# Weight projections with the token columns read and written from last to first

## The reference

```
z   = h @ w_in                                   # 2048 x 11272
y_r = retention_out @ w_ret_proj                 # 1024 x 2048
y_f = attention_out @ w_fox_proj                 # 1024 x 2048
mix = (sigmoid(gr) * y_r + sigmoid(gf) * y_f) @ w_out
x1  = layer_norm(ALPHA * h + mix)
ffn = (silu(x1 @ w1) * (x1 @ w3)) @ w2           # inner width 5632
ple = sigmoid(x1 @ w_pg) * (p @ w_pe)
y   = layer_norm(ALPHA * x1 + ffn + ple)
```

## Time and profile before

| | |
|---|---|
| median of three runs | 1943.95 us (1942.95 to 1946.54) |
| span of the profiled execution, first to last instruction | 1944.3 us |
| TensorE matmul busy | 1859.9 us, 96% |
| VectorE busy | 1050.1 us, 54% |
| ScalarE busy | 793.6 us, 41% |
| GpSimd busy | 148.5 us, 8% |
| mean granted TensorE clock | 0.981 of full speed |

### The profile page before, as it was taken

The page is one execution under the profiler, slowest core; times in us unless marked ns, Lnnn a source line. Parts: engine busy times, 40 slices in busy tenths (PEclk is TensorE's granted clock), DMA queues, the critical chain, the costliest instruction groups (busy, mean ns, idle before and its releaser), DMA issues.

```text
span 1944.3 us, 39410 instructions
## 1 busy us (share of the span) xinstructions
PE 1859.9 (96%) x14346; PEld 1754.6 (90%) x14346; DVE 1050.1 (54%) x2097; ACT 793.6 (41%) x930; POOL 148.5 (8%) x262
## 2 busy tenths in 40 slices
PE   5999999999899999999978999999999999999996
PEld 4999998888777877889978999999999999999995
DVE  5444575864767666447556554444444444444554
ACT  2444434433433443334335445555433343443333
POOL 3330101111121112000000000000000000000000
PEclk9999999999999999899988999999999999999999
DMA  5555677787799899545533555555555555555551
GB/s 157 151 160 158 215 247 227 249 273 228 260 344 315 294 333 334 166 149 183 181 106 125 180 177 181 182 182 179 177 179 178 183 180 182 177 179 173 178 179 45
DMA packets 318257, 386.18 MB, mean 199 GB/s; under 512 B 16376, under 2 KB 293368, under 8 KB 317784
## 3 DMA queue, kind: packets, MB, share of 16 engines
q1 hardware_dynamic: 286832, 287.48, 47.7%
q0 software_dynamic: 28352, 95.84, 14.3%
q10 hardware_dynamic: 2992, 1.79, 0.4%
HBM read 371.21 MB, written 13.84 MB: 198 GB/s over the span
## 4 chain that ended last, share of the span: by engine, by line
PE 72%; DVE 4%; issue 2%; DMA 2%; ACT 1%; POOLq 0%; DVEq 0%; ACTq 0%; POOL 0%
PE acc L506 22%; PE acc L511 22%; PE acc L507 22%; PE X L631 2%; DMA page<-in_cache_v 2%; PE X L756 1%; PE X L819 1%; DVE pagesum L1249 1%; PE X L620 1%; PE X L641 0%; DVE uT L1497 0%; DVE wlo L452 0%; PE X L613 0%; ACT uT L1078 0%; ACT whi L447 0%
## 5 line engine op out<-in xcount | busy, mean ns | idle before, releaser
L452 DVE TENSOR_TENSOR wlo<-raw,whi 128x1024 fp32r<-128x1024 f32 (+1 forms) x552 | 658.9, 1202 | 658.5 <-ACT whi L447 651.5
L447 ACT ACTIVATE whi<-raw 128x1024 fp32r<-128x1024 f32 (+1 forms) x552 | 568.8, 1037 | 683.2 <-PE acc L511 680.8
L506 PE MATMUL acc<-x_hi,whi 128*128 128x264 f32 x1664 | 415.8, 285 | 10.3 <-DVE x_lo L1506 6.8
L507 PE MATMUL acc<-x_lo,whi 128*128 128x264 f32 x1664 | 415.2, 285 | 0.0
L506 PE MATMUL acc<-hT_hi,whi 128*128 128x264 f32 x1408 | 366.8, 295 | 0.0
L507 PE MATMUL acc<-hT_lo,whi 128*128 128x264 f32 x1408 | 356.8, 288 | 0.0
L506 PEld LDWEIGHTS acc<-x_hi,whi 128*128 128x128 f32 x1664 | 313.8, 189 | 11.4 <-issue 7.2
L507 PEld LDWEIGHTS acc<-x_lo,whi 128*128 128x128 f32 x1664 | 315.3, 189 | 0.0
L506 PEld LDWEIGHTS acc<-hT_hi,whi 128*128 128x128 f32 x1408 | 270.5, 192 | 41.5 <-issue 37.9
L507 PEld LDWEIGHTS acc<-hT_lo,whi 128*128 128x128 f32 x1408 | 271.4, 193 | 0.1
L511 PE MATMUL acc<-x_hi,wlo 128*128 128x264 f32 x1664 | 239.7, 286 | 0.0
(11 more groups left out here) (300 smaller groups left out, 1727.3 us busy)
## 6 DMA issues: line engine op xcount, KB each, us to landing
raw<-in_w SPq DMA_DIRECT2D x256, 512.0 KB, 3.9
raw<-in_w_in SPq DMA_DIRECT2D x176, 512.0 KB, 4.9
page<-in_cache_k POOLq DMA_DIRECT2D x64, 512.0 KB, 6.2
page<-in_cache_v POOLq DMA_DIRECT2D x64, 512.0 KB, 5.7
raw<-in_w_out SPq DMA_DIRECT2D x32, 512.0 KB, 4.5
raw<-in_w_pg SPq DMA_DIRECT2D x32, 512.0 KB, 3.5
stateS<-in_state_ret POOLq DMA_DIRECT2D x8, 1024.0 KB, 7.9
out_ret_state_sample<-stateS POOLq DMA_DIRECT2D x8, 1024.0 KB, 7.3
```

The lines of the kernel that those rows point to most:

```text
L447: nc.scalar.activation(whi[:, s, 0:k, :], raw[:, s, 0:k, :], ACT.Copy).then_inc(S["hi_made"], 1)
L452: nc.vector.tensor_tensor(wlo[:, s, 0:k, :], raw[:, s, 0:k, :], whi[:, s, 0:k, :].bitcast(F32), ALU.subtract).then_inc(S["lo_made"], 1)
L506: mm(acc[c.acc][:, m, 0:T], w, xh[:, c.kt0 + t, :], start=c.first and t == 0, stop=False)
L507: mm(acc[c.acc][:, m, 0:T], w, xl[:, c.kt0 + t, :], start=False, stop=False)
```

## The change

In `multiply` every moving operand and every PSUM target goes through a helper that turns the free axis around. Column 263 is read first and column 0 last; the result of column 263 is written to column 263. The same products are summed in the same places, in the same number of instructions.

```
+            def backward(ap):
+                return ap[:, ::-1]
+
...
-                        mm(acc[c.acc][:, m, 0:T], w, xh[:, c.kt0 + t, :], start=c.first and t == 0, stop=False)
-                        mm(acc[c.acc][:, m, 0:T], w, xl[:, c.kt0 + t, :], start=False, stop=False)
+                        mm(backward(acc[c.acc][:, m, 0:T]), w, backward(xh[:, c.kt0 + t, :]), start=c.first and t == 0, stop=False)
+                        mm(backward(acc[c.acc][:, m, 0:T]), w, backward(xl[:, c.kt0 + t, :]), start=False, stop=False)
...
-                        last = mm(acc[c.acc][:, m, 0:T], wlo[:, s, t, m * P:(m + 1) * P], xh[:, c.kt0 + t, :],
+                        last = mm(backward(acc[c.acc][:, m, 0:T]), wlo[:, s, t, m * P:(m + 1) * P], backward(xh[:, c.kt0 + t, :]),
                                   start=False, stop=c.last and t == c.n_kt - 1)
```

## The result

The changed kernel took 1931.14 us in the median of four runs (1926.86 to 1936.93), the kernel before 1944.06 (1942.95 to 1946.54). The ratio is 0.9934, with a 95% interval from 0.9914 to 0.9954: faster by 0.7%, some 13 us. The forecast was 1944 with a range from 1936 to 2100.

The account below looks back on a forecast made before the run. TensorE's projection matmuls were taken to bound the kernel, any change in their cost being paid in full. All terms were 0 on the 1944.3 us span, giving 1944 us, with a range from 1,936 to 2,100.

Parts of the forecast that it names:

- What bounds the kernel, and the 12,960 x 0.122: TensorE's weight projections: 12,960 matmuls at 0.122 us each make 1,581 us, 81% of the span, paid in full.
- Instructions and waits at 0: Same matmuls, order and semaphores, and the same distance between writing and adding to a column; both terms 0.
- The write and add into PSUM at step -1: Writing projection results to PSUM columns backward; taken as 0, with bounds of -10 and +100 ns a matmul.
- The read of the moving row at step -1: Reading each projection matmul's moving row backward; taken as 0, with bounds of -10 and +100 ns a matmul.
- a collision of the weight load with the moving row that another order of addresses avoids: Projection matmuls lose the 10 ns between 112 and 122; faster rival, 1,814 us at best, chance 0.05.
- a part of it more likely than the whole: Said of the faster rival: losing part of the 10 ns a matmul is likelier than losing all 130 us.
- The nearest row: Bias of the past: matmuls with eight separate runs per row, whose address jumps were free; used as evidence for 0.
- Moving alone wants about 112: From the norm sums' 222 ns a record: moving alone about 112 ns, loading weights about 113, both together 122.
- Half the pace: Slower rival: backward float32 neighbours go singly, two cycles a column, +100 ns a projection matmul, 3,210 us; chance 0.14.
- a fixed cost: Slower rival: each backward matmul pays once at its start; 10 ns visible gives +130 us, 2,074; chance 0.09.
- four cycles: Slower rival: each element waits for a full access in both memories, 444 ns a matmul, some 6,100 us; chance 0.02.
- the 10 ns which I took for a possible cover: In the fixed-cost rival, up to 9 or 10 ns a matmul could hide, since moving alone wants 112 of 122.

Follow-up runs that it names:

- e1: Changed kernel with only the moving rows read backward and PSUM columns written ascending; 1931.72 us, ratio 0.9944 to the kernel before.
- e5: Changed kernel, weight ring split into halves 128 bytes apart, low part of g shifted 64 bytes; moving rows mostly 128 to 224 bytes after weights modulo 256; 1928.04 us, ratio 0.9917.
- e6: As e5 with even and odd weight slots swapped, so moving rows start 0 to 96 bytes after weight rows modulo 256; 1939.36 us, ratio 0.9976.
- e9: Changed kernel, backward, with weight rows spaced 1056 bytes instead of 1024, like activation rows, and low part of g as in e5; 1928.05 us, ratio 0.9913.
- e11: As e9, backward, with the activations and all behind them moved 64 bytes; 1948.54 us, ratio 1.0018 to the kernel before.
- e8: As e4, backward, with 288 moving columns instead of 264 in each projection matmul; 2058.55 us in one run, step 132.04 ns.
- e12: The layout of e9, read and written forward; 1928.98 us, ratio 0.9926 to the kernel before.
- e7: The layout of e5, read and written forward; 1951.25 us, ratio 1.0038 to the kernel before.
- e4: As e3, but rows read and columns written backward; 1929.86 us in one run, step 120.99 ns.
- e3: Kernel before, forward, each chunk reading its moving columns from its operand's first two row blocks at one of eight starting places; 1933.43 us in one run.

## Why the prediction was wrong

- *What bounds the kernel, and the 12,960 x 0.122.* Right. TensorE has no idle time in the long stage, and the gain is the change of the step times the count: 11.3 to 12.4 us computed, 12.9 in the medians.
- *Instructions and waits at 0.* Right: the counts and the work of the other engines are unchanged, and the idle time from 200 to 900 us moved by 1.5 us, the other way.
- *"The write and add into PSUM at step -1 ... I take 0."* Right, by itself: 1.0007.
- *"The read of the moving row at step -1 ... I take 0."* This is the step that failed. Its bounds held (-10 to +100 ns); the value was -0.96, and e1, with the read alone turned, has all of it. What comes nearest to the cause stood there as the lower bound, "a collision of the weight load with the moving row that another order of addresses avoids", and was dismissed in the rivals with "their meeting doesn't depend on a direction" and with the argument that the distance of addresses changes all the time. It does change, and it comes back every two chunks; each place costs its own amount, and the amounts depend on the direction. That the cost is a collision isn't shown; that it depends on both addresses is (e5 against e6, e9 against e11). Since "a part of it more likely than the whole" was said there, the range should have reached below 1936 by such a part.
- *The nearest row.* The bias of the past did what it was used for, since nothing halved the pace, but it has two cycles a column and couldn't speak about one nanosecond.
- *"Moving alone wants about 112."* The row didn't show that. Each record of the norm sums has a weight load of its own (64 loads for 64 matmuls at L819), and 112 is half of a record at two cycles a column. By that row the excess over the columns is 2 ns where the columns are slow; in the projections it is 10 and more. So the 10 ns between 112 and 122 had no row behind them.
- *What I didn't look at.* The starts of before, to the nanosecond, already had the pattern of two kinds of chunk at 122.8 and 121.4. A step that isn't constant under constant work says that something beside the columns enters.
- *Half the pace, a fixed cost, four cycles.* None came. e8 shows that the 10 ns which I took for a possible cover are no cover: they stand on top of the columns.

The Trainium skill's rule on 16-byte lines ("Advanced Engine Details and Errata", "SBUF Cachelines") fits a backward read without a loss. Its rule on PSUM ("PSUM Cachelines" there) doesn't reach this case: a descending pair isn't slowed, ratio 1.0007. And its page "TensorE: Matmul & The Clock Gate" ("Step-by-step: what each phase is for") says that weights for the next matmul load by a read port of their own and don't steal SBUF read bandwidth from the running one. Here the step moved by 0.84 ns when only weight buffers were moved (e5, e6), so at this scale the two aren't independent.

What is shown: the gain comes by the read side alone; the step depends on the addresses of moving rows and of weights modulo 256; and what direction is worth depends on them, from nothing (e9, e12) to 1.7 ns (e5, e7). What stays open: the rule that gives a step from addresses, and what else enters, since e7 has two steps at the same addresses. Distance within a matmul (A1) and distance to the next weights (A4) each foretold some steps and missed others.

## What to carry to other kernels

Where TensorE is never idle, compare starts to the nanosecond over a repeating unit of work: a pattern in them that repeats with the addresses may be time to be had from the layout, here 1% with the kernel before as the base, by spacing weight rows like activation rows and shifting the activations by 192 bytes. A direction or an order of access isn't fast or slow by itself; before it is kept, try the same layout both ways. With thousands of equal instructions on the path, a range has to allow a nanosecond for each in both directions.

## What the runs showed of the hardware

- A one-pass float32 matmul of 128 x 128 by 264 columns at full clock took 120.0 ns in the quietest places and up to 124.8 as a mean in the worst (e4), against 110 ns of columns; single steps ranged from 115 (before) to 133 (e12). In stretches at 1.2 GHz it took 220, the columns alone (before and changed).
- Moving the weight buffers alone by 128 bytes modulo 256 changed the step from 120.89 to 121.73 ns (e5, e6); moving the activations and all that lies behind them by 64 bytes, from 120.65 to 122.30 (e9, e11).
- Backward, 6 of 8 places were quiet at 120.0 to 120.1 ns (e4); forward two had a mean of 120.0, in the second part of a chunk only (e3).
- In one layout read forward, the same chunks at the same addresses took 122.1 ns a matmul in one stretch and 122.9 in a later one (e7).
- Writing PSUM columns in descending order cost nothing (1944.60 us, ratio 1.0007).
- With 288 columns the step was 132.0 ns, by place 131.1 to 133.4 (e8), against 120 ns of columns: what stands over the columns doesn't shrink as they grow.
